# RWKV scan on four quarter tiles: r's operands in four arrays, stored by another queue, and crosswise tiles for the second direction

## The reference, cut to what matters

```python
def rwkv7_scan(r, w, k, v, kk, b_vec, s0):
    def step(state, inp):
        r_t, w_t, k_t, v_t, kk_t, b_t = inp
        sa = -jnp.einsum('bhvk,bhk->bhv', state, kk_t)
        state = (state * w_t[:, :, None, :] + sa[..., None] * b_t[:, :, None, :]
                 + v_t[..., None] * k_t[:, :, None, :])
        return state, jnp.einsum('bhvk,bhk->bhv', state, r_t)
    ...
```

## Time and profile before

| | us |
|---|---|
| runs | 4085.94, 4098.98, 8352.19; median 4098.98 |
| profiled execution | 4086.96 |
| its span | 4085.2 |
| PE busy in the span | 3546.5 |
| DVE busy | 2125.1 |
| POOL busy | 787.5 |
| ACT busy | 677.0 |

### The profile page before, as it was taken

The page is one execution under the profiler, slowest core; times in us unless marked ns, Lnnn a source line. Parts: engine busy times, 40 slices in busy tenths (PEclk is TensorE's granted clock), DMA queues, the critical chain, the costliest instruction groups (busy, mean ns, idle before and its releaser), DMA issues. The chain is left out here.

```text
span 4085.2 us, 63947 instructions
## 1 busy us (share of the span) xinstructions
PE 3546.5 (87%) x28192; PEld 2841.4 (70%) x28192; DVE 2125.1 (52%) x2296; ACT 677.0 (17%) x1103; POOL 787.5 (19%) x819
## 2 busy tenths in 40 slices
PE   6999999999998989799999999985566545778798
PEld 3777777777887878688888888853455434678476
DVE  2577777733335555554543443275778643321464
ACT  2122222312000001211110100021223101221100
POOL 0111111111000000061024052002655766000000
PEclk8999999999999999899999999987788767888899
DMA  9444444444233452322322233267356699764142
GB/s 391 149 154 145 160 150 145 150 172 174 98 119 121 175 189 100 114 82 87 108 97 83 86 121 110 95 236 230 116 177 201 210 206 190 186 209 154 72 170 108
DMA packets 290469, 616.56 MB, mean 151 GB/s; under 512 B 117496, under 2 KB 184176, under 8 KB 258448
## 3 DMA queue, kind: packets, MB, share of 16 engines
q1 hardware_dynamic: 186736, 427.49, 31.9%
q0 software_dynamic: 21936, 95.56, 7.2%
q10 hardware_dynamic: 81520, 89.42, 6.6%
HBM read 472.02 MB, written 140.39 MB: 150 GB/s over the span
## 5 line engine op out<-in xcount | busy, mean ns | idle before, releaser
L180 PE MATMUL front_ps<-b_hT,p_wb 128*128 128x512 f32 x4224 | 980.6, 392 | 6.8 <-PEq L94 6.8
L180 PEld LDWEIGHTS front_ps<-b_hT,p_wb 128*128 128x128 f32 x4224 | 790.7, 188 | 187.9 <-issue 20.6
L1770 PE MATMUL in_ps<-b_hT,in_wb 128*128 128x512 f32 (+1 forms) x3264 | 750.7, 390 | 13.3 <-DVE in_wb L1757 13.3
L1770 PEld LDWEIGHTS in_ps<-b_hT,in_wb 128*128 128x128 f32 (+1 forms) x3264 | 607.0, 187 | 148.2 <-DVE in_wb L1757 13.5
L1755 DVE CAST in_wb<-in_raw 128x2048 fp32r<-128x2048 f32 (+1 forms) x68 | 82.7, 1215 | 536.3 <-PE in_ps L1770 531.4
L168 DVE CAST p_wb<-p_raw 128x2048 fp32r<-128x2048 f32 x88 | 108.0, 1227 | 431.8 <-PE front_ps L180 421.0
L811 POOL DMA_DIRECT2D front_mwb<-in_w_ada x128 | 101.0, 794 | 796.1 <-PE front_mps L821 791.1
L1770 PEld LDWEIGHTS in_ps<-b_hc,in_wb 128*128 128x128 f32 (+1 forms) x1728 | 211.4, 189 | 3.2
L1770 PE MATMUL in_ps<-b_hc,in_wb 128*128 128x256 f32 (+1 forms) x1728 | 212.6, 283 | 0.0
L170 DVE TENSOR_TENSOR p_wb<-p_raw,p_wb 128x2048 fp32r<-128x2048 f32 x88 | 201.8, 2293 | 3.0
L1209 PE MATMUL mid_ps<-mid_wb,b_hT 128*128 128x512 f32 x768 | 178.0, 392 | 13.5 <-DVE mid_wb L1194 13.5
(11 more groups left out here) (446 smaller groups left out, 4757.0 us busy)
## 6 DMA issues: line engine op xcount, KB each, us to landing
p_raw<-in_w_in_tiles SPq DMA_DIRECT2D x88, 1024.0 KB, 6.2
in_raw<-in_w_in_tiles SPq DMA_DIRECT2D x67, 1024.0 KB, 4.8
front_mwb<-in_w_ada POOLq DMA_DIRECT2D x128, 512.0 KB, 5.0
r_scr<-rprep_ob ACTq DMA_DIRECT2D x16, 2694.0 KB, 13.5
scan_rops<-r_scr SPq DMA_DIRECT2D x24, 1796.0 KB, 11.2
open_wb<-in_w_ada_groups SPq DMA_DIRECT2D x32, 1024.0 KB, 11.4
g_scr<-gprep_ob SPq DMA_DIRECT2D x8, 3474.0 KB, 11.5
merge_raw<-in_w_branch_units SPq DMA_DIRECT2D x32, 512.0 KB, 4.5
```

Source lines behind the costliest of these rows:

```text
L180: last = self.nc.tensor.matmul(self.ps[:, n % 2, :], self.wb[:, n % 2, x, kt, :], self.hT[:, y, kt, :], start=kt == term == 0, stop=kt == ...
L1770: last = self.nc.tensor.matmul(self.ps[0:width, n % 3, first:end], self.wb[:, n % 2, x, kt, 0:width], h[:, y, kt, :], start=kt == term == ...
```

## The change

- `r_scr` is split in four arrays (`R_PARTS`), each contiguous per step: home (decay repeated in 4 columns, M_AK, A: 132 columns, 12 chunks), read (R, 64 columns, the 8 latent chunks), turn (B, K, 128 columns, 12 chunks), mix (M_RB, M_RK, 128 columns, 8 chunks). For d = 1, turn and mix are stored with their 64-partition halves swapped.
- A store is 8 DMAs (2 of N, 6 of parts) instead of 3 and is issued by SyncE, in the order load of pairs 0 to 2, then for each i: store (i,0), load i+3, store (i,1).
- The scan loads the parts that a step needs: 8 DMAs (home, turn, values per direction, and d = 1's values once more with swapped halves), and 4 more (read, mix) in output steps.
- For d = 1 the products of keys, advance, value outputs and rest outputs go crosswise: rows of one half of the array to the columns of the other. The loops take q outside and d, h inside, so that four quarter tiles follow each other. `values` and the state part of the outputs stay straight.
- Keys are split: the value part of step k+1 is issued at the end of step n (waits for the loads and both state adds), the state part at the head of the next. Outputs are split in three, with one bank for each direction; the second is the delta scan's `po`. The result of `middle` goes to a part of the delta scan's middle bank, with waits added around it.
- For d = 1, DVE does the negation and the copy. The update is one for both directions (two adds, one decay); the outputs are added after it (`collect`), which also frees the operands.

```diff
-R_COLS = 8 * C + 1
+
+R_AT = 4
+
+R_PARTS = (("home", C, R_AT + 2 * C, NCH), ("read", R_AT + 3 * C, C, T // C), ("turn", R_AT + 4 * C, 2 * C, NCH),
+           ("mix", R_AT + 6 * C, 2 * C, T // C))
+R_COLS = R_AT + 8 * C
...
+        mask = self.k.mask[:, d].unsqueeze(1).to_broadcast([P, NCH, 2, C])
+        first = self.ob(i, d)[:, :, col:col + C]
+        both = bass.AP(first.tensor, first.offset, [first.ap[0], first.ap[1], [other - col, 2], first.ap[2]])
+        self.tt(both, self.ps_m[:].rearrange("p (c j t) -> p c j t", j=2, t=C), mask)
...
-    def store(self, act_e, i, d):
-
-        act_e.wait_ge(self.s["m_out"], 4 * i + 2 * d + 2)
+    def store(self, sp, i, d):
+
+        ob, done = self.ob(i, d), self.stored[(2 * i + d) % 3]
+        sp.wait_ge(self.s["k_out"], 2 * i + d + 1)
+        sp.wait_ge(self.s["m_out"], 4 * i + 2 * d + 2)
         for h in range(2):
             rows = self.systems[d, NCH * GH:SYS, :].rearrange("(q h c) (s t) -> (q h) s c t", c=NCH, h=2, t=C)
-            act_e.dma_start(rows[2 * i + h:2 * i + h + 1].rearrange("q s c t -> (q s) c t"),
-                            self.ob(i, d)[64 * h:64 * h + 64, :, 0:C]).then_inc(self.stored[(2 * i + d) % 3], 16)
-        act_e.dma_start(self.r_scr[:, d, :, i:i + 1].rearrange("c p q x -> p (c q) x"), self.ob(i, d)[:, :, C:R_COLS]).then_inc(self.stored[(2 * i + d) % 3], 16)
+            sp.dma_start(rows[2 * i + h:2 * i + h + 1].rearrange("q s c t -> (q s) c t"),
+                         ob[64 * h:64 * h + 64, :, 0:C]).then_inc(done, 16)
+        for name, col, width, n in R_PARTS:
+            to = self.r_scr[name][:, d, :, i:i + 1].rearrange("c p q x -> p (c q) x")
+            x = ob[:, 0:n, col:col + width]
+            if name in ("home", "read"):
+                sp.dma_start(to, x).then_inc(done, 16)
+            elif d == 0:
+                for c in (slice(0, n // 2), slice(n // 2, n)):
+                    sp.dma_start(to[:, c], x[:, c]).then_inc(done, 16)
+            else:
+
+                for h in range(2):
+                    sp.dma_start(to[64 - 64 * h:P - 64 * h], x[64 * h:64 * h + 64]).then_inc(done, 16)
...
                 m.load_all(sp)
+                for i in range(3):
+                    m.load(sp, i)
                 for i in range(RP):
-                    m.load(sp, i)
+                    m.store(sp, i, 0)
+                    if i + 3 < RP:
+                        m.load(sp, i + 3)
+                    m.store(sp, i, 1)
...
+    LOADS = 16 * 8
 
     def load(self, sp, k):
         u = k % 2
         if k >= 2:
 
             sp.wait_ge(self.s["free"], k - 1)
+        c = [STEPS[k][d] for d in range(2)]
         for d in range(2):
-            c = STEPS[k][d]
-            sp.dma_start(self.ops[:, u, d], self.r_scr[c, d]).then_inc(self.loaded[u], 16)
-            sp.dma_start(self.val[:, u, d], self.v_scr[c]).then_inc(self.loaded[u], 16)
+            for name in ("home", "turn"):
+                sp.dma_start(self.parts[name][:, u, d], self.r_scr[name][c[d], d]).then_inc(self.loaded[u], 16)
+            sp.dma_start(self.val[:, u, d], self.v_scr[c[d]]).then_inc(self.loaded[u], 16)
+        sp.dma_start(self.val[64:P, u, 2], self.v_scr[c[1], 0:64]).then_inc(self.loaded[u], 16)
+        sp.dma_start(self.val[0:64, u, 2], self.v_scr[c[1], 64:P]).then_inc(self.loaded[u], 16)
+        if STEPS[k][2]:
+            for d in range(2):
+                for name in ("read", "mix"):
+                    sp.dma_start(self.parts[name][:, u, d], self.r_scr[name][c[d], d]).then_inc(self.shown[u], 16)
...
+    def term(self, bank, q, h, lhs, rhs, at, first, end):
+
+        r, to = slice(64 * at, 64 * at + 64), slice(64 * h, 64 * h + 64)
+        return self.nc.tensor.matmul(bank[to, q * C:(q + 1) * C], lhs[r, q], rhs[r, q], start=first and q == 0, stop=end and q == RP - 1)
...
+    def value_keys(self, pe, k):
+
+        u = k % 2
+        pe.wait_ge(self.loaded[u], self.LOADS * (k // 2 + 1))
+        if k > 0:
+
+            pe.wait_ge(self.s["added"], k)
         for q in range(RP):
-            for n, (lhs, rhs) in enumerate(terms):
+            for d in range(2):
                 for h in range(2):
-                    r = slice(64 * h, 64 * h + 64)
-                    last = self.nc.tensor.matmul(bank[r, q * C:(q + 1) * C], lhs[r, q], rhs[r, q],
-                                                 start=n == 0, stop=n == len(terms) - 1)
-        return last
-
-    def part(self, k, d, col):
-        return self.ops[:, k % 2, d, :, col:col + C]
-
-    def keys(self, pe, k):
-
-        u = k % 2
+                    self.term(self.work[d], q, 1 - h if d else h, self.part(k, d, self.M_AK), self.val[:, u, d], h, True, False)
...
+    def state_keys(self, pe, k):
         if k == 0:
             pe.wait_ge(self.s["init"], 1)
-        pe.wait_ge(self.loaded[u], 64 * (k // 2) + 64)
-        for d in range(2):
-
-            pe.wait_ge(self.s["s_out"], 2 * k + d + 1)
-            self.heads(self.work[d], ((self.part(k, d, self.A_), self.state[:, d]),
-                                      (self.part(k, d, self.M_AK), self.val[:, u, d]))).then_inc(self.s["w_ok"], 1)
+        else:
+            pe.wait_ge(self.s["s_out"], k)
+        for q in range(RP):
+            for d in range(2):
+                for h in range(2):
+                    last = self.term(self.work[d], q, 1 - h if d else h, self.part(k, d, self.A_), self.state[:, d], h, False, True)
+        last.then_inc(self.s["w_ok"], 1)
...
+    def advance(self, pe, k):
+        u = k % 2
+        for d in range(2):
+            pe.wait_ge(self.v_ok[d], k + 1)
+        for n, col in enumerate((self.B_, self.K_)):
+            for q in range(RP):
+                for d in range(2):
+                    for h in range(2):
+                        rhs = self.val[:, u, 2 * d] if n else self.y[:, d]
+                        last = self.term(self.work[d], q, h, self.part(k, d, col), rhs, 1 - h if d else h, n == 0, n == 1)
+        last.then_inc(self.s["st_ok"], 1)
...
+    def update(self, dve, k):
+        nc, u, link, state = self.nc, k % 2, self.link, self.state
+        dve.wait_ge(self.s["st_ok"], k + 1)
+        for d in range(2):
+            link(nc.vector.tensor_tensor(state[:, d], state[:, d], self.wide(self.work[d]), ALU.add))
+        dve.sem_inc(self.s["added"], 1)
+        decay = self.parts["home"][:, u, :, :, 0:1].to_broadcast([P, 2, RP, RD])
+        link(nc.vector.tensor_tensor(state[:], state[:], decay, ALU.mult))
+        dve.sem_inc(self.s["s_out"], 1)
...
+                        r.state_keys(pe, n - LAG)
+                        if STEPS[n - LAG][2]:
+                            if n == NCH:
+                                pe.wait_ge(g.s["o_out"], 4 * (T // C))
+                            r.state_outputs(pe, n - LAG)
                     if in_g(n + 1):
+                        if in_r(n):
+
+                            pe.wait_ge(r.s["inv_ok"], 4 * (n - LAG) + 4)
                         g.middle(pe, n + 1)
                     if in_r(n + 1):
                         r.middle(pe, n + 1 - LAG)
@@ -3660,18 +3750,27 @@
                     if in_r(n):
                         r.values(pe, n - LAG)
                     if in_g(n + 1):
+                        if in_r(n + 1):
+                            pe.wait_ge(r.s["mid_ok"], n + 2 - LAG)
                         g.offdiagonal(pe, n + 1)
                     if in_r(n + 1):
                         r.offdiagonal(pe, n + 1 - LAG)
-                    for half in range(2):
-                        if in_g(n):
-                            g.advance(pe, n, half)
-                        if in_r(n):
-                            r.advance(pe, n - LAG, half)
+                    if in_r(n) and STEPS[n - LAG][2]:
+                        r.value_outputs(pe, n - LAG)
+                    if in_g(n):
+                        g.advance(pe, n, 0)
+                    if in_r(n):
+                        r.advance(pe, n - LAG)
+                    if in_g(n):
+                        g.advance(pe, n, 1)
+                    if in_r(n) and STEPS[n - LAG][2]:
+                        r.rest_outputs(pe, n - LAG)
                     if n >= NCH:
                         out.fold(pe, n - NCH)
                     if n > NCH:
                         out.add(pe, n - NCH - 1)
+                    if in_r(n + 1):
+                        r.value_keys(pe, n + 1 - LAG)
```

More of the change, by code:

```diff
@@ L3238, with __init__ @@
 class RwkvScan:
-    M_RB, M_AK, M_RK, A_, R_, B_, K_ = (n * C for n in range(7))
-    def __init__(self, nc, st, r_scr, v_scr, systems, oT):
+    A_, R_, M_AK, M_RB, M_RK, B_, K_ = (("home", R_AT + C), ("read", 0), ("home", R_AT), ("mix", 0), ("mix", C), ("turn", 0), ("turn", C))
+    def __init__(self, nc, st, r_scr, v_scr, systems, oT, px, po):
         self.nc, self.r_scr, self.v_scr, self.systems, self.oT = nc, r_scr, v_scr, systems, oT
-        self.ops = st.sb("rops", [P, 2, 2, RP, R_COLS - C])
```

(36 more changed lines are left out.)

130 lines of the change are left out of this document (65 added, 65 removed).

## The result

The changed kernel runs in 4057.97 us (median of four, 4055.16 to 4060.49); against the runs of the kernel before the ratio is 0.9926 (95% interval 0.9909 to 0.9942). Its profiled execution took 4055.16 us, 31.8 less than the 4086.96 of the one before. Forecast were 4015 us and 72 us of gain. Less than half of that came. The time lies inside the range given (3950 to 4075) and on the forecast side, but the size of the main term was wrong.

What follows compares the result with a forecast made beforehand. Taken as bounds: r's start hangs on the landing of pair 3's stores, r-only steps on PE's instruction fetch. Preparation 20, joint steps 16 and r-only steps 36 make 72 us; 4087 - 72 = 4015 us, range 3950 to 4075.

Steps and rivals of the forecast that it cites:

- Stores from ACT to SyncE: Preparation: ACT freed of issuing stores, so POOL and r start earlier; 15 us of gain, ends 0 and 36.
- the parts: Preparation stores: fewer bytes in more, smaller packets; 5 us of gain, ends 60 of loss and 10 of gain.
- The bounds for the packets: Preparation: 57344 more packets priced at the mean cost 163 us of DMA time, 81 ahead of POOL.
- DVE in the preparation: Preparation: DVE's mask and end copies change little; taken as 0, ends 0 and 0.3 us a pair.
- loads of the scan: Scan: more DMAs and later inverse loads, needed a step or more later; taken as 0, without cover 3 us a step.
- waits and copies: Scan: DVE copies beside ACT and one update for both directions; taken as 0, ends 1 gained and 2 lost a step.
- Hidden: Scan loads: the later inverse loads are covered because they are needed a step or more later, 28 us.
- Four tiles: Scan: four tiles halve product time; 3.8 us gained a context step, 5.7 an output step; ends nothing and all.
- rival B: Scan: crosswise tiles take turns at loading; only the preparation's 20 us and 10 for lighter loads stay; 4057 us, chance 0.14.
- What the fetch lets through: Steps of r alone: instruction supply in blocks of 256 limits the tiles' gain to 4.5 us a step, 36 us in all.
- the term 3.2 x 3.5: Steps of r alone: 3.2 blocks of 256 instructions after the first two, expected at about 3.5 us each.
- Joint steps: Steps with delta scan and r together: the delta scan's waits take part; 4.0 x 4 = 16 us, ends 0 and 24.

Runs made afterwards that it cites:

- spstore: The kernel before with one edit: the preparation's stores (3 DMAs each, one array) issued by SyncE in the changed kernel's order; 4065.93 us, ratio 0.9955.
- straight: The changed kernel with d = 1 on the straight tiles too, two tiles at a time, data laid out accordingly; 4068.29 us, ratio 0.9952.
- noload: The changed kernel without the operand loads of the last six RWKV steps (older data used again, inverses still loaded); 4017.76 us, ratio 0.9828.
- narrow: The changed kernel with each 64x64x64 product of the RWKV scan streaming 16 columns instead of 64, same number of instructions; 4074.30 us, ratio 0.9967.
- tiny: The changed kernel with each of the 12 operand DMAs moving one head pair of eight in the last six RWKV steps; 4024.06 us, ratio 0.9842.
- poolload: The changed kernel with the RWKV operand loads from step 2 on issued by GpSimd in its software queue instead of SyncE; 4053.42 us, ratio 0.9912.
- spread: The changed kernel with the read and mix loads issued half a step later, so loads run in two bursts; 4057.05 us, ratio 0.9916.
- pad64: The changed kernel with 64 unused columns (256 B) behind each head pair's part in the DRAM arrays, giving smaller load rows; 4038.05 us, ratio 0.9878.
- base: The changed kernel as it is, against the kernel before: ratio 0.9926; run again beside some of the experiments 0.9917.

## Why the prediction was right or wrong

*Stores from ACT to SyncE: right.* 15 us and 5 for the parts were forecast. POOL's start moved by 20.9 us and r's by 16.1, and spstore gives 19 us for the move alone. The split was wrong in the small: the parts gave nothing, the move all of it. The bounds for the packets were far too wide: the queue's share of 0.49 over 444 us is 218 us of DMA time where it had been 180, so the finer stores cost 38 us of it, not 163. r's start moved 5 us less than POOL's because POOL lost some of its lead again: its four batches of r start 20.9, 19.1, 18.7 and 15.3 us earlier than before.

*DVE in the preparation, loads of the scan, waits and copies: right as far as no semaphore wait was added.* PE waits for none of them in the steps of r alone. But "Hidden" and "taken as 0" for the scan loads were right only for the change, since the new loads beside the old ones made no difference that could be measured (straight 4068, spstore 4066). In the step itself they cost 7 us (noload), and that was the largest thing to be had here. I had seen it in the earlier trace rows and used it only to cap the gain.

*Four tiles: right as to whether, wrong as to worth.* The keys run at twice the rate, as L2363's loads allowed; rival B's turns did not happen. The Trainium skill's rule ("TensorE: Matmul & The Clock Gate", part 3, the mechanism) did not keep four tiles from twice the rate at full clock. That the loads of two tiles over the same rows take turns is compatible with what was measured: at a clock of 0.50 narrow's four tiles took 0.106 us for four matmuls and four loads, just two of the 54 ns that L2363's loads had at that clock. With 64 columns streamed, at 0.061 us for four and four, no cost of it shows.

*"What the fetch lets through": the step that failed.* 4.5 us a step were forecast for r alone, between 2.7 and 6.6; 0.6 came. The cap, the number of blocks and the near 4 us of an undisturbed one were right: noload gives 3.9, and the changed kernel's window 4.00 (with PE busy for 3.49 of it at half clock). Mis-sized was the term 3.2 x 3.5 and what it is held against. I took the first two blocks at their lengths under load and all the rest at 3.5 us, less than any block in the rows. The distances between q8's packets in the seven steps show what came instead: 12 late ones of 7.8 us on average before and 14 of 7.3 after, two a step in both; and the others 4.2 us on average before and 4.1 after. 3.5 is about the least distance, not the usual one, and straight tiles had used the blocks nearly as fast as they came. There was next to nothing to win in them.

I also left out the clock. In the seven steps, in which PE stood idle for 57.4 us instead of 35.7, the granted clock was 0.78 for 0.86, and 0.71 in the step that took 32.1 us. With straight tiles, PE busy 156 us of 194, it was 0.88. PE's own work would have gained 40 us over the seven steps by my figures (7 x 5.7); 26 came at the lower clock, and 22 of these went into idle time.

*Joint steps: right in kind, 9.9 us for 16.* They are where four tiles pay: 7.7 us against straight tiles. There the delta scan's wider products (fewer instructions for the same work) stand between r's, so that PE doesn't use a block as fast as one comes. The packets agree: the distances up to 6 us were 4.75 us on average before and 4.6 in straight, longer than in the steps of r alone (4.2 and 4.05), and 4.1 with four tiles. No run tested the reason by itself.

*Rival B had the number (4057) and not the mechanism.* Its time is the sum with the tiles' gain at nothing and some 10 us for lighter loads. In fact the loads' bytes gave nothing measurable (straight against spstore, 4068 and 4066) and crosswise tiles gave those 10. That the number fits is luck.

What stays open: why a packet of instructions starts late while large rows move. It isn't the number of DMAs or of their packets (tiny), not the queue of the loads (poolload), not that they come in one burst (spread), and not the packet's own 1.1 us. It is the loads' bytes (noload, and tiny against pad64) and partly their rows' size (pad64 against base). That the fetch waits at a DMA engine behind whole rows would fit all five runs, but what holds back its start was not seen.

## What to carry to other kernels

Where PE runs long lists of small matmuls, count its instructions before its columns: here a packet of 256 records of matmul and load came every 3.8 to 3.9 us on average with no loads beside it, and never sooner than 3.3 us after the last. Where PE already works at that pace, a faster shape of tile bought idle time, at a lower clock. Shorten the list, or shield its supply: breaking the large rows of the background loads into ones of 256 to 528 B took 16 to 20 us off here, once those of 256 and 512 B began at multiples of 256 B. DMAs with many packets are not free for the engine that issues them; a queue whose engine has nothing else to do took 19 us off a critical chain, and moving the finer ones back cost 63.

## What the hardware showed that I had not expected

A background load slows an engine that never waits for it: 7 us of a 27.1 us step. Rows of 512 B instead of 4 KB raise the DMA share from 0.66 to 0.82 or 0.87 and shorten the step all the same. Packets of 512 B at a pitch of 528 B took the store queue from 49.0% to 64.5% of the DMA engines' time, with nearly the same bytes and packets; at 768 B it was 48.6%. No run tells whether multiples of 256 B are needed or of something smaller. And with 16 columns streamed instead of 64 the granted clock was 0.51 for 207 us on end, so that less work took longer.
